# 64-wide attentions of a two-model kernel: both heads of a tile in one step, in a new order

## The reference, cut to what matters

```python
# mixer_b of the first model: 16 heads, 4 groups of keys, a band of 128 keys, a learned sink per head
o, _ = banded_window_attention(q, k, v, B_WINDOW - 1, B_HEAD_DIM ** -0.5, sink=...)
# memory_cross_attention, in both layers: 4 heads over 256 memory tokens
s = jnp.einsum('bshd,bmhd->bhsm', q, k).astype(jnp.float32) * MEM_HEAD_DIM ** -0.5
p = jax.nn.softmax(s, axis=-1)
o = jnp.einsum('bhsm,bmhd->bshd', p, v.astype(jnp.float32))
# the second model: 16 heads, 4 groups of keys, three branches over the same queries (compressed keys,
# selected keys, a window), each a masked softmax, their outputs summed with sigmoid gates per head
```

## Time and profile before

| | us |
|---|---|
| median of 3 runs | 2417.02 (2410.09 to 2423.25) |
| the profiled execution | 2415.6 |
| its span | 2413.8 |
| TensorE busy | 2273.4 (94% of the span) |
| DVE, ScalarE, GpSimd busy | 1298.2, 921.1, 250.7 |
| chain that ended last: TensorE's share | 83% |

### The profile page before, as it was taken

One profiled execution on the slowest core, in us unless ns is written; L12 is line 12 of the kernel. 1 busy time (PEld: TensorE's weight loads), 2 busy tenths in 40 slices (PEclk: granted clock), 3 DMA queues, 4 the chain that ended last, 5 costly groups with the idle time before them and its releaser, 6 DMA issues.

```text
span 2413.8 us, 34422 instructions
## 1 busy us (share of the span) xinstructions
PE 2273.4 (94%) x10882; PEld 1855.7 (77%) x10882; DVE 1298.2 (54%) x2537; ACT 921.1 (38%) x1850; POOL 250.7 (10%) x143
## 2 busy tenths in 40 slices
PE   7986999999999799999999999999999689999997
PEld 6675777888888687788888888888887667777766
DVE  5876444666644566466664454555544643545443
ACT  4433453322322266432223332222223334555551
POOL 0042221000001111110000210000002000011112
PEclk8998999999999999999999999999999889999888
DMA  3121111332333110223232332222222312000001
GB/s 131 51 88 53 61 53 62 96 101 90 104 102 102 66 36 26 77 90 99 93 104 96 104 97 96 99 99 96 96 96 79 113 63 85 2 19 9 19 10 70
DMA packets 50053, 182.93 MB, mean 76 GB/s; under 512 B 5552, under 2 KB 5680, under 8 KB 49840
## 3 DMA queue, kind: packets, MB, share of 16 engines
q1 hardware_dynamic: 49824, 181.35, 22.9%
q0 software_dynamic: 144, 0.52, 0.1%
HBM read 179.76 MB, written 2.10 MB: 75 GB/s over the span
## 4 chain that ended last, share of the span: by engine, by line
PE 83%; DVE 7%; issue 4%; ACT 3%; POOL 1%; DMA 1%; DVEq 0%; ACTq 0%; POOLq 0%; SPq 0%
PE pj L1863 68%; PE ps L2006 4%; PE po L2062 4%; PE pt L2022 2%; ACT w_hi L670 1%; DMA raw<-in_wstream 1%; PE po L2047 1%; PE ps L2176 1%; DVE s_sb L1303 1%; PE pj L1973 1%; DVE rtmp L1248 1%; DVE w_lo L1118 1%; PE po L2071 1%; ACT p_sb L757 1%; DVE rtmp L1245 1%
## 5 line engine op out<-in xcount | busy, mean ns | idle before, releaser
L1863 PE MATMUL pj<-h_hi,w_hi 128*128 128x512 f32 x1736 | 706.9, 407 | 21.0 <-DVE w_lo L1118 15.6
L670 ACT ACTIVATE w_hi<-raw 128x1024 fp32r<-128x1024 f32 x334 | 353.7, 1059 | 865.6 <-PE pj L1863 848.8
L1863 PE MATMUL pj<-h_lo,w_hi 128*128 128x512 f32 x1736 | 683.8, 394 | 0.0
L1863 PE MATMUL pj<-h_hi,w_lo 128*128 128x512 f32 x1736 | 683.6, 394 | 0.0
L1118 DVE TENSOR_TENSOR w_lo<-raw,w_hi 128x1024 fp32r<-128x1024 f32 x288 | 390.4, 1356 | 392.2 <-ACT w_hi L670 391.9
L1863 PEld LDWEIGHTS pj<-h_hi,w_hi 128*128 128x128 f32 x1736 | 331.1, 191 | 90.1 <-issue 17.1
L1863 PEld LDWEIGHTS pj<-h_hi,w_lo 128*128 128x128 f32 x1736 | 330.5, 190 | 71.1
L1863 PEld LDWEIGHTS pj<-h_lo,w_hi 128*128 128x128 f32 x1736 | 331.5, 191 | 64.6 <-issue 1.4
L1863 PE MATMUL pj<-G_hi,w_hi 128*128 128x512 f32 x704 | 278.1, 395 | 3.1 <-DVE G_lo L1367 3.0
L1863 PE MATMUL pj<-G_lo,w_hi 128*128 128x512 f32 x704 | 276.0, 392 | 0.0
L1863 PE MATMUL pj<-G_hi,w_lo 128*128 128x512 f32 x704 | 275.9, 392 | 0.0
(11 more groups left out here) (295 smaller groups left out, 2531.4 us busy)
## 6 DMA issues: line engine op xcount, KB each, us to landing
raw<-in_wstream SPq DMA_DIRECT2D x334, 512.0 KB, 3.4
xT<-in_x SPq DMA_DIRECT2D x4, 512.0 KB, 9.5
out_x<-xT SPq DMA_DIRECT2D x4, 512.0 KB, 2.7
memT<-in_mem SPq DMA_DIRECT2D x1, 1024.0 KB, 12.3
cst<-in_cst SPq DMA_DIRECT2D x1, 512.0 KB, 10.5
tab<-in_tab POOLq DMA_DIRECT2D x1, 512.0 KB, 5.0
posi<-in_pos SPq DMA_DIRECT2D x1, 256.0 KB, 2.8
vec<-in_vec SPq DMA_DIRECT2D x1, 182.5 KB, 2.4
```

The costliest lines, as they stand in the source:

```text
L670: nc.scalar.activation(w_hi[:, c.par * CW:(c.par + 1) * CW], raw[:, c.par * CW:(c.par + 1) * CW], ACT.Copy).then_inc(hi_ready, 1)
L1863: mm = nc.tensor.matmul(acc, w[:, col:col + P], x[part], start=first and k == 0, stop=last and k == 2)
```

## The change

The four 64-wide attentions get a class of their own, `Pairs`, and run in steps: one step is a branch and a query block for both heads; 4 steps to a tile in amem, bmem and bq, 9 in nq. In nq the eight cmp units become one step: each head has four score products of 32 columns in one bank, then one reduction for all, one exponential for both heads, one transpose a head, and one product a head with `cmp_v` laid out as a block diagonal of 4 x 64 columns.

- Keys are stored once. The first head's scores read rows 0 to 63 and go to `ps[0]`, the second head's read rows 64 to 127 and go to `ps[1]`. The zeroing of `b_k` and `n_k` goes.
- TensorE's order: scores of step k+1, a projection block, the values of step k-1, the transposes of step k (in bq one more projection block).
- ScalarE's order: the copies of step k, then the exponentials of step k+1. Up to 256 columns both heads lie in one bank `pt[0]` and are copied at once.
- `ps`, `s_sb`, `p_sb` and `pt` hold one step, a half for each head; the transposed exponentials have two buffers by step (`pT` and `pT1`).
- The output is turned in step 1 of the next tile, split in steps 2 and 3, the rope is in steps 1 and 2 (bq) or 4 and 5 (nq), and the branch sums, gates and the splits of the weight chunks move with them.

The diff, cut to the new step functions:

```diff
+class Pairs:
+    def __init__(self, name, tiles, branches, first_step, first_tile, first_pass, out0):
+        self.name, self.tiles, self.dv, self.scale, self.m = name, tiles, 64, 64.0 ** -0.5, 8
+        self.steps = [(branch, b) for branch in branches for b in (range(1) if branch == "cmp" else range(NB))]
+        self.first_step, self.first_tile, self.first_pass, self.out0 = first_step, first_tile, first_pass, out0
+        self.n, self.passes = len(self.steps), len(branches)
+        self.ends = [max(k for k, (name_, _) in enumerate(self.steps) if name_ == branch) for branch in branches]
+        self.at_rope = {"bq": 1, "nq": 4}.get(name)
+        self.at_refill = {"bq": 1, "nq": 7}.get(name, 3)
...
-            pool.wait_ge(x_ready, RESIDUALS["down0"] + DT)
-            nc.gpsimd.memset(b_k[:, :], 0.0).then_inc(zeroed, 1)
             splits("bq")
...
-            nc.gpsimd.memset(n_k["win"][:, :], 0.0)
-            nc.gpsimd.memset(n_k["slc"][:, :], 0.0).then_inc(zeroed, 1)
+            nc.gpsimd.memset(cmp_v[:, :], 0.0).then_inc(zeroed, 1)
...
+            def pair_softmax(ph, i, j, k):
...
+                w = ph.keys(k)[1]
+                p = ph.pass_at(k)
+                g = bank_of(ph, j, p)
+                act.wait_ge(pair_turned, s)
+                if branch == "cmp":
+                    act.wait_ge(pair_max, s * 2 + 2)
+                    settle(act)
+                    nc.scalar.activation(pc[:, :], s_sb[:, 0:2 * P], ACT.Exp, scale=ph.scale).then_inc(pair_exp, 2)
+                    return
+                for hh in range(2):
+                    act.wait_ge(pair_max, s * 2 + (hh + 1))
+                    settle(act)
+                    r = b * 2 + hh
+                    if ph.name == "bq":
+                        h = (i * 2 + j) * 2 + hh
+                        nc.scalar.activation(of_pass(esink, g, r), nsink[:, sl(h, 1)], ACT.Exp, scale=-1.0,
+                                             bias=ST(NEGM, hh))
+                    nc.scalar.activation(p_sb[:, hh * S:hh * S + w], s_sb[:, hh * S:hh * S + w], ACT.Exp,
+                                         scale=rsm[:, b:b + 1] if branch == "mem" else ph.scale, bias=ST(NEGM, hh),
+                                         accum_out=sums_at(ph, j, p, r)).then_inc(pair_exp, 1)
+            def pair_bring(ph, i, j, k):
+                s = step_of(ph, i, j, k)
+                w = ph.keys(k)[1]
+                dst = turned[(j * ph.n + k) % 2]
+                act.wait_ge(pair_turned, s + 1)
+                if not isinstance(s, int) or s > 1:
+                    act.wait_ge(pair_valued, s - 1)
+                settle(act)
+                if w <= MEM:
+                    nc.scalar.activation(dst[:, 0:2 * w], pt[0][:, 0:2 * w], ACT.Copy).then_inc(pair_copied, 2)
+                    return
+                for hh in range(2):
+                    nc.scalar.activation(dst[:, hh * S:hh * S + w], pt[hh][:, 0:w], ACT.Copy).then_inc(pair_copied, 1)
+            def pair_tile(ph, i, j):
+                for k in range(ph.n):
+                    pair_bring(ph, i, j, k)
+                    pair_softmax(ph, i, j, k + 1)
+                    if k == 2 and not (isinstance(i, int) and j == 0):
+                        output_hi(ph, i, j - 1)
+                    if k == ph.at_refill and more(ph, i, j) and (
+                            ph.name == "bmem" or ph.name != "amem" and not (isinstance(i, int) and j == 0)):
+                        split_hi(query_at(ph, i, j + 1)[0] + 2)
+                    if k == ph.n - 1 and ph.name == "bq":
+                        query(ph, i, j + 2)
...
+            def pair_maximum(ph, i, j, k):
...
+                s = step_of(ph, i, j, k)
+                branch, b = ph.steps[k]
+                w = ph.keys(k)[1]
+                if branch == "cmp":
+                    dve.wait_ge(pair_scored, s * 2 + 2)
+                    dve.wait_ge(pair_exp, s * 2)
+                    settle(dve)
+                    for hh in range(2):
+                        nc.vector.tensor_tensor(s_sb[:, hh * P:(hh + 1) * P], ps[hh][:, 0:P], C("cmp", 0, P),
+                                                ALU.add).then_inc(pair_taken, 1)
+                    dve.wait_ge(pair_taken, s * 2 + 2)
+                    each = s_sb[:, 0:2 * P].rearrange("p (u n) -> p u n", u=8)
+                    link(nc.vector.tensor_reduce(cmx[:, :], each, mybir.AxisListType.X, ALU.max))
+                    nc.vector.tensor_tensor(each, each, cmx[:, :].unsqueeze(2).broadcast_to([P, 8, NCMP]),
+                                            ALU.subtract).then_inc(pair_max, 2)
+                    return
+                for hh in range(2):
+                    dve.wait_ge(pair_scored, s * 2 + (hh + 1))
+                    if not isinstance(s, int) or s > 0:
+                        dve.wait_ge(pair_exp, s * 2 + (hh - 1))
+                    settle(dve)
+                    nc.vector.tensor_tensor_reduce(out=s_sb[:, hh * S:hh * S + w], in0=ps[hh][:, 0:w], in1=bias(branch, b),
+                                                   scale=1.0, scalar=-3.0e38,
+                                                   op0=ALU.mult if branch == "mem" else ALU.add, op1=ALU.max,
+                                                   accum_out=ST(MX, hh)).then_inc(pair_taken, 1)
+                    dve.wait_ge(pair_taken, s * 2 + (hh + 1))
+                    if ph.name == "bq":
+                        h = (i * 2 + j) * 2 + hh
+                        done = nc.vector.tensor_scalar(ST(NEGM, hh), ST(MX, hh), -ph.scale, nsink[:, sl(h, 1)],
+                                                       ALU.mult, ALU.min)
+                    elif branch == "mem":
+                        done = nc.vector.tensor_scalar(ST(NEGM, hh), ST(MX, hh), rsm[:, b:b + 1], -1.0, ALU.mult, ALU.mult)
+                    else:
+                        done = nc.vector.tensor_scalar(ST(NEGM, hh), ST(MX, hh), -ph.scale, None, ALU.mult)
...
+            def pair_tile(ph, i, j):
+                first = isinstance(i, int) and j == 0
+                for k in range(ph.n):
+                    pair_maximum(ph, i, j, k + 1)
+                    if k == 0 and not first:
+                        scale_pass(ph, i, j - 1, ph.passes - 1)
+                    if k - 1 in ph.ends[:-1]:
+                        scale_pass(ph, i, j, ph.ends.index(k - 1))
+                    if k == 1 and ph.name == "nq" and not first:
+                        gate_output(ph, i, j - 1)
+                    if k == 3 and ph.name != "nq" and not first:
+                        output_lo(ph, i, j - 1)
+                    if more(ph, i, j) and ph.at_rope is not None and k in (ph.at_rope, ph.at_rope + 1):
+                        query(ph, i, j + 1, k - ph.at_rope)
+                    if k == ph.n - 1 and ph.name == "nq" and ahead(ph, i, j):
                         take_query(ph, i, j + 2)
-                    if last and p == 0:
-                        if v == ph.at_gate and ph.name == "nq":
-                            gate_output(ph, *last[:2])
-                        if v == ph.at_lo:
-                            output_lo(ph, *last[:2])
...
+            def pair_scores(ph, t, k):
+                if k == ph.n:
+                    t, k = t + 1, 0
+                if t == ph.tiles:
+                    return
+                branch, b = ph.steps[k]
+                s, par, g = step_of(ph, 0, t, k), t % 2, t // 2
+                k0, w = ph.keys(k)
+                if k == 0:
+                    if branch == "mem":
+                        at = query_at(ph, 0, t)[1]
+                        pe.wait_ge(pj_free[at.par], at.half + 2)
+                    else:
+                        pe.wait_ge(roped, RP[ph.name] + t + 2)
+                if s:
+                    pe.wait_ge(pair_taken, 2 * s)
+                else:
+                    pe.wait_ge(score_taken, ATT["aq"].first_score + ATT["aq"].tiles * ATT["aq"].n + 2)
+                for hh in range(2):
+                    rows = slice(hh * 64, hh * 64 + 64)
+                    if branch == "cmp":
+                        for c in range(NB):
+                            mm = nc.tensor.matmul(ps[hh][:, c * NCMP:(c + 1) * NCMP],
+                                                  qn[rows, par * S + c * P:par * S + (c + 1) * P],
+                                                  cmp_k[rows, g * NCMP:(g + 1) * NCMP], start=True, stop=True)
+                    else:
+                        q = qn if branch == "mem" else qs
+                        if branch == "mem":
+                            keys = mem_k[0 if ph.name == "amem" else 1][rows, t * MEM:(t + 1) * MEM]
+                        else:
+                            keys = (b_k if branch == "band" else n_k[branch])[rows, g * S + k0:g * S + k0 + w]
+                        mm = nc.tensor.matmul(ps[hh][:, 0:w], q[rows, par * S + b * P:par * S + (b + 1) * P], keys,
+                                              start=True, stop=True)
```

(67 more changed lines are left out.)

334 lines of the change are left out of this document (167 added, 167 removed).

## The result

The changed kernel takes 2423.62 us (median of 20 runs), the kernel before 2417.49 (20 runs): ratio 1.003, 95% interval 1.0019 to 1.0042. I had forecast 2391 with a range up to 2420. The profiled execution has a span of 2426.5 us against 2413.8, 12.7 more.

What follows compares the result with a forecast made beforehand. TensorE was taken as the bound. nq -28 - 5.7 + 0, bq +11.5, memory +6.2, fills and drains +4 and scores -14 gave -26 us: 2391 against the median 2417.0; 8-in-10 range 2358 to 2420.

Steps and rivals of the forecast that it cites:

- clock term for nq alone: nq: of 31 us lost to half clock, 3 would remain, -28 us; lowest all 31 back, highest none.
- bq +11.5: bq: 32 steps' row switches +9.6, merged values +2.9, rope +2, small copy waits -3; sum +11.5 us.
- the rope: bq: its second half ends about 0.3 us after TensorE wants the next tile's first scores, +2 us.
- merged values: bq: merging two groups of value products costs 0.09 us, 32 times, +2.9 us.
- Memory +6.2: amem and bmem: 16 steps at 0.39 us each, +6.2 us, with nothing coming back from idle time.
- waits -5.7: nq: of 14.4 us of TensorE waits, 7.7 go and 2 are new in the two last tiles, -5.7 us.
- rival (2): nq: clock not kept, thin short steps at each tile's start; about 6 of 28 us return, 2413 us; chance 0.18.
- Scores -14: All four attentions: second head's first pass overlaps first head's last; half of 28.5 us taken, -14 us.
- rival (1): All four attentions: the two heads' scores overlap fully, 14 us more come back, 2377 us; chance 0.24.
- forecast 34 to 36: nq: its eight tiles take 34 to 36 us between their turns of the output, the last two 29 to 30.
- Switch 0.3 us a step: Steps scoring on 64 rows: each visit to part of the array costs 0.3 us, +2.7 a tile in nq.
- Rival (3): Single p_sb: copy and exponential loop stalls 120 steps; gain gone from 0.21 us each, 2439 at 0.4; chance 0.14.

Runs made afterwards that it cites:

- 1: Changed kernel with bq's rope one step earlier, in steps 0 and 1 of a tile: 2399.17 us, 0.993 of the kernel before.
- 5: Changed kernel with four repairs: bq's rope earlier, nq's rope earlier, nq's weight chunk rounded earlier, both memory attentions on all rows: 2353.67 us, ratio 0.973 to before.
- 2: Changed kernel with amem alone scoring over all 128 rows, keys padded with zeros for each head: 2417.16 us, 0.9997 of the kernel before.
- 9: 5 with bq's and nq's slc and win scores on all 128 rows, amem's heads both on the first 64: 2371.12 us, ratio 0.9828 to before.
- 4: Changed kernel with each score product of the two memory attentions issued twice into the same bank: 2410.14 us, 0.9968 of the kernel before.
- 8: 5 with a step's transposes ahead of the preceding step's values on TensorE: 2340.84 us, 0.9694 of the kernel before.
- 7: 5 with both heads' scores on the same first 64 rows in bq and in nq's slc and win: 2388.28 us, 0.9907 of the kernel before.
- 11: Changed kernel with only a step's transposes put ahead of the preceding step's values on TensorE: 2406.28 us, 0.9956 of the kernel before.

## Why the prediction was wrong

**The step that failed is the clock.** The sum has a clock term for nq alone, -28; bq and the memory attentions were priced from rows at full clock, as if they would keep it. In nq 8.8 us came back instead of 28, and bq and the memory attentions lost 17.0 and 31.7 us to half clock instead of 1.2 and 4.5, 43 us that the sum doesn't have, against a miss of 33 in the medians. The second step that failed is the waits. The sum's terms beside what the two sets of windows show for all four attentions, in us:

| | forecast | measured |
|---|---|---|
| half clock | -28 | +34 (nq -9, bq +16, memory +27) |
| TensorE idle (waits, rope, fills) | -3 | +35 (nq +19, bq +12, memory +4) |
| TensorE's work at full clock | +5 | -56 (nq -42, bq -7, memory -7) |
| sum | -26 | +13 |

That nq as a whole came near its forecast (31.4 us shorter for 42.7) is luck: clock and waits gave 44 us less than I took, and the work fell by 33 more.

- **bq +11.5 (with scores: +8.3); measured +20.4.** The mis-sized term is the rope: "it ends about 0.3 us behind ... +2". I saw that the split slows a rope operation to 1.42 us on average and took that average. But the split met a whole addition, 2.73 us, and TensorE waited 2.25 us, 13.6 in all, and half clock followed each time. Without that (1, 5) bq is 6 to 7.5 us shorter than before. The merged values were no cost that shows: with all rows a tile is 13.59 against 14.83.
- **Memory +6.2 (with scores: +4.4); measured +24.0.** Its mechanism was missing: at 64 rows the stage stays at the half clock that it falls to near its start for some 24 us or to its end (bmem in 2, amem in 9), and with all rows for some 4; bmem didn't even fall to it in the kernel before and in 4. With all rows and the transposes in front (8) the two stages are 3.1 us above before.
- **nq clock -28 and waits -5.7.** The wait for GpSimd's sum went, nearly as argued, but the maximum behind the rope (14.5 us in seven tiles) and the split (5.0) took its place, and 22.8 us of half clock stayed. That is rival (2)'s outcome, about 9 of the 28 came back where it has 6, but not its mechanism: the waits stand in front of win's 512 keys and of the projection, and are not short steps at a tile's start. With both gone (5) the clock is 0.99 and a steady tile 30.7 us, below the forecast 34 to 36: 1.7 us because the overlap saves more than I took, 1.1 because a change of rows costs less, and some 0.5 that no run splits further.
- **Scores -14: too small.** 0.14 to 0.20 us a block, where I took 0.06: for the 216 blocks of bq and nq, 11.2 + 23.0 = 34 us (7 against 5), beyond the 28.5 that rival (1) has for all 248 blocks; that rival was right in kind, and its time failed with the clock.
- **Switch 0.3 us a step: about right.** 0.20 in nq, 0.37 in bq.
- **Rival (3), the single p_sb, fell.** Transposes wait for exponentials 1.3 us in all of nq even in 8, where they have no values in front of them as cover. The slower side came by another way, which I had not listed.
- **Order.** I took the values in front of the transposes as cover for the exponentials and priced no cost. It costs 12.8 us (8) to 17 (11).
- **Readings.** Of the slices with an 8 only 38 and 39 lie in nq; 34 and 37 show a 9. The four attentions fill 490 us and not 480. Nothing in the sum rests on either.

Why half clock lasts so long with 64-row scores stays open. Nor was bq tried on all rows with each head's keys padded by zeros, as amem in 2: the padded keys need space that the second buffer of turned exponentials takes.

## What to carry to other kernels

Price the granted clock in every stage that a change touches, also in those that ran at full clock before: waits of 2 us once a tile and scores on half of the rows, with the half clock that followed, cost here more (69 us) than the work that was saved (56). When steps are regrouped, the side work placed by step number (rope, refill, split) has to be placed anew; lay each such operation beside GpSimd's long splits, by its slowest case and not by its mean. And try a reordering on its own: of the two here one was worth 10 us and the other cost 13, and the best kernel (2340 us, 3.1% below before) has only the first.

## What was unexpected of the hardware

- At half clock, with scores from 64 rows, TensorE busy in every window (2.00 of 2.00 us) stayed at half clock for 30 us, and for 10 more to the stage's end; with scores from 128 rows it came back to full within some 4 us (9 and 2). The steps have the same instructions; 2's padded keys add rows of zeros. Issuing the 64-row scores twice brought it back too (4): adding TensorE work made the kernel 13 us faster. The Trainium skill (TensorE: Matmul & The Clock Gate, Part 1) lets the gate follow how busy TensorE has been; bq agrees, where half clock followed each wait of some 2.3 us, and 9 against 2 shows that busy time alone doesn't decide.
- Two products from different halves of the rows ran almost wholly together: 1.06 us for a pair that takes 1.91 from the same rows. That is what the Trainium skill (TensorE: Matmul & The Clock Gate, Part 3: Packing small matmuls) says; the change back to 128 rows takes away 0.20 to 0.37 us of it a step.
- VectorE's addition of 128x512 took 2.73 us beside a GpSimd subtraction of 2.65 us, which it outlasted by 0.55 us; the multiplication ahead of it took 0.68 us, though the same subtraction began 0.43 us before its end.
